# TensorE's seven-pass loop of the recurrence written out, its value transposes moved behind the round's first product, and each stage's semaphores cleared inside the next stage

## The reference, cut to what matters

```python
def step(S, inp):                      # chunks of tokens
    qt, kt, vt, gt = inp
    G = jnp.cumsum(gt, axis=2)
    o_inter = jnp.einsum('bhtk,bhkv->bhtv', qt * jnp.exp(G), S)
    A = jnp.einsum('bhtk,bhtsk->bhts', qt, decay * kt[:, :, None, :, :])
    o = o_inter + jnp.einsum('bhts,bhsv->bhtv', A, vt)
    S = jnp.exp(G_last)[..., None] * S + jnp.einsum('bhsk,bhsv->bhkv', kt * jnp.exp(G_last - G), vt)
    return S, o
```

## Time and profile before

| | |
|---|---|
| runs, us | 2702.21, 2703.32, 2710.44 |
| profiled execution, its own time | 2706.89 us |
| its span, first to last instruction | 2705.1 us |
| mean granted TensorE clock | 0.954 |
| busy: PE, PEld (weight load) | 2440.8 us, 2263.8 us |
| busy: DVE (VectorE), ACT (ScalarE), POOL | 1252.1, 1035.6, 432.7 us |
| stage hgrn2, first product to the first of the next stage | 563.1 to 1410.8 us |

### The profile page before, as it was taken

One profiled execution on the slowest core, in us unless ns is written; L12 is line 12 of the kernel. 1 busy time (PEld: TensorE's weight loads), 2 busy tenths in 40 slices (PEclk: granted clock), 3 DMA queues, 4 the chain that ended last, 5 costly groups with the idle time before them and its releaser, 6 DMA issues. The chain is left out here.

```text
span 2705.1 us, 59385 instructions
## 1 busy us (share of the span) xinstructions
PE 2440.8 (90%) x25397; PEld 2263.8 (84%) x25397; DVE 1252.1 (46%) x1639; ACT 1035.6 (38%) x1505; POOL 432.7 (16%) x282
## 2 busy tenths in 40 slices
PE   5999899999999999999948996982899999999993
PEld 4999899999899899899948996971788888888882
DVE  4123210015555555555542112027567676677673
ACT  4222221113333233233322112132566666676663
POOL 1221131111111111111103113102111212111110
PEclk9999999999999999999969997986899999999997
DMA  3112231211101101101014225135487887878774
GB/s 117 32 36 79 97 104 50 68 41 41 35 22 46 35 17 51 35 17 51 19 43 143 76 71 214 31 118 233 167 315 281 301 306 276 306 285 315 271 275 173
DMA packets 183594, 351.02 MB, mean 130 GB/s; under 512 B 10512, under 2 KB 110864, under 8 KB 183440
## 3 DMA queue, kind: packets, MB, share of 16 engines
q1 hardware_dynamic: 177296, 327.78, 34.1%
q0 software_dynamic: 6144, 20.98, 3.0%
HBM read 301.54 MB, written 47.19 MB: 129 GB/s over the span
## 5 line engine op out<-in xcount | busy, mean ns | idle before, releaser
L1598 DVE TENSOR_TENSOR ex_w_lo<-ex_raw,ex_w_hi 128x1024 fp32r<-128x1024 f32 x377 | 450.1, 1222 | 150.8 <-ACT ex_w_hi L1590 147.6
L1590 ACT ACTIVATE ex_w_hi<-ex_raw 128x1024 fp32r<-128x1024 f32 x384 | 398.9, 1057 | 143.9 <-PE ex_out L1832 122.0
L176 PE MATMUL hg_proj<-trunk_h_hi,hg_w_hi 128*128 128x320 f32 x768 | 251.7, 328 | 16.8 <-issue 16.8
L177 PE MATMUL hg_proj<-trunk_h_lo,hg_w_hi 128*128 128x320 f32 x768 | 243.9, 318 | 0.3 <-issue 0.2
L178 PE MATMUL hg_proj<-trunk_h_hi,hg_w_lo 128*128 128x320 f32 x768 | 243.4, 317 | 0.0
L1830 PE MATMUL ex_out<-ex_w_hi,ex_x_hi 128*128 128x512 f32 x512 | 205.6, 402 | 2.2 <-DVE ex_x_lo L1616 2.2
L1831 PE MATMUL ex_out<-ex_w_hi,ex_x_lo 128*128 128x512 f32 x512 | 200.5, 392 | 0.0
L1832 PE MATMUL ex_out<-ex_w_lo,ex_x_hi 128*128 128x512 f32 x512 | 200.2, 391 | 0.0
L176 PEld LDWEIGHTS hg_proj<-trunk_h_hi,hg_w_hi 128*128 128x128 f32 x768 | 150.3, 196 | 20.2 <-issue 18.2
L176 PE MATMUL hg_proj<-trunk_h_hi,trunk_w_hi 128*128 128x320 f32 x512 | 161.9, 316 | 5.3 <-POOLq L201 5.3
L177 PE MATMUL hg_proj<-trunk_h_lo,trunk_w_hi 128*128 128x320 f32 x512 | 158.8, 310 | 0.0
(11 more groups left out here) (329 smaller groups left out, 6108.8 us busy)
## 6 DMA issues: line engine op xcount, KB each, us to landing
ex_raw<-in_w_exp_gate_dram SPq DMA_DIRECT2D x32, 2048.0 KB, 11.4
ex_raw<-in_w_exp_up_dram SPq DMA_DIRECT2D x32, 2048.0 KB, 12.4
ex_raw<-in_w_exp_down_dram SPq DMA_DIRECT2D x32, 2048.0 KB, 17.8
trunk_w_raw<-in_w_in_dram SPq DMA_DIRECT2D x48, 512.0 KB, 4.2
hg_w_raw<-in_w_in_dram SPq DMA_DIRECT2D x16, 512.0 KB, 4.7
ya<-gm_ya SPq DMA_DIRECT2D x8, 640.0 KB, 3.4
m_a<-ma_m SPq DMA_DIRECT2D x8, 640.0 KB, 3.4
yb<-hg_Kt_b SPq DMA_DIRECT2D x8, 640.0 KB, 5.1
```

The source lines that it names most:

```text
L176: nc.tensor.matmul(out, self.hi[s][:, k, :], x_hi[:, k, c], start=(k == 0), stop=False)
L177: nc.tensor.matmul(out, self.hi[s][:, k, :], x_lo[:, k, c], start=False, stop=False)
L1590: nc.scalar.activation(w_hi[u % RING][:], src, ACT.Copy).then_inc(s["w_hi_ready"], 1)
L1598: ops.tensor_tensor(w_lo[u % RING][:], src, w_hi[u % RING][:].bitcast(F32), ALU.subtract).then_inc(s["w_lo_ready"], 1)
```

## The change

1. TensorE's `Fori` over heads 0 to 6 becomes a Python loop: its seven passes stand one behind the other in the program. The other engines keep their loops.
2. `pe_values` and `act_values` go from the end of a round (head g+1) to the place behind the first product group of the next (head g). The wait for `v` moves from DIAG to level 6 (INNER), where the bank area that held the transposed values is first written again; DIAG waits for the query tile instead.
3. A stage's semaphores are no longer cleared behind its own block but at the end of POOL's program in the following block, and are returned to the allocator after that block; those of the last stage are cleared at the end of the program, as before.

```diff
@@ class Stage @@
+    used = []
     def __exit__(self, *a):
-        if self.sems and a[0] is None:
-            for sem in self.sems:
-                self.nc.gpsimd.sem_clear(sem)
-                self.nc.release_semaphore(sem)
+        if a[0] is None:
+            Stage.used += self.sems
         return self.ctx.__exit__(*a)
+    @contextmanager
     def block(self):
-        return self.nc.Block()
+        before, Stage.used = Stage.used, []
+        with self.nc.Block() as block:
+            yield block
+            @block.gpsimd
+            def _(pool):
+                for sem in before:
+                    self.nc.gpsimd.sem_clear(sem)
+        for sem in before:
+            self.nc.release_semaphore(sem)
@@ hgrn2, pe_step @@
             if j == DIAG:
-                pe.wait_ge(s["v_ready"], g + 1)
+                W.moved(pe, g, TQ)
...
+                if j == INNER:
+                    pe.wait_ge(s["v_ready"], g + 1)
@@ hgrn2, pe_round (act_round likewise, with act_values) @@
                     W.multiply(nc, pe, *tiles[n // PARTS], n % PARTS, h_hi, h_lo)
+                if g is not None and n == 0:
+                    pe_values(pe, g)
                 if g is not None and n < STEPS:
                     pe_step(pe, g, n)
-            if tiles[-1][1] == TI:
-                pe_values(pe, tiles[-1][0])
@@ hgrn2, block.tensor @@
-                with pe.Fori(0, HEADS - 1) as g:
+                for g in range(HEADS - 1):
                     pe_round(pe, tiles_with(g), g)
```

More of the change, by code:

```diff
@@ L14 @@
-from contextlib import ExitStack
+from contextlib import ExitStack, contextmanager
 import concourse.bass as bass
@@ L71, in __exit__, with clear_all @@
     def __exit__(self, *a):
-        if self.sems and a[0] is None:
-            for sem in self.sems:
-                self.nc.gpsimd.sem_clear(sem)
-                self.nc.release_semaphore(sem)
+        if a[0] is None:
+            Stage.used += self.sems
         return self.ctx.__exit__(*a)
+    def clear_all(self):
+        for sem in Stage.used:
+            self.nc.gpsimd.sem_clear(sem)
+            self.nc.release_semaphore(sem)
+        Stage.used = []
     def sb(self, name, shape, dt=F32):
@@ L675, in act_round @@
                     act_move(act, r, t, n % PARTS)
+                if g is not None and n == 0:
+                    act_values(act, g)
                 if g is not None:
                     act_gla(act, g, n)
-            if tiles[-1][1] == TI:
-                act_values(act, tiles[-1][0])
         def pool_round(pool, tiles):
@@ L2051, in build @@
         norm_out(nc, C, x3, I["final_g"], y_prompt, y_sample)
+        top.clear_all()
 _INS = ["x_prompt", "x_sample", "norm1_g", "w_in", "a_vnorm_g", "a_spatial_w", "a_spatial_b", "b_lb_logits",
```

## The result

The changed kernel takes **2667.76 us** (median of four runs, 2664.53 to 2671.03), the kernel before, run beside it, 2706.8 us. The ratio is 0.9857, with a 95% interval of 0.9831 to 0.9882: faster by some 39 us, where 45.9 us were predicted. The forecast was a median of 2657 us, in a range of 2648 to 2668 us. The profiled execution took 2670.59 us, 36.3 us less than that of before (2706.89). The direction was right; the gain was about a sixth smaller than the working gave.

A forecast was written before the change was run, and what follows sets the result against it. TensorE's queue was taken to bound the recurrence's rounds, with jumps costing pauses and low clock. 35.1 + 4.8 - 0.5 + 6.5 = 45.9 us off a 2703.3 us median gave 2657 us, range 2648 to 2668 us.

The forecast's parts named there:

- What bounds the kernel: Recurrence rounds are as long as TensorE's queue; each of six jumps back costs a code pause (16.8 us in all) and low clock.
- Part 1: Recurrence loop written out: six rounds fall from 612.81 to 577.74 us, 35.1 us gained, bounds 16.8 and 38.3.
- I cost the fetching in line at nothing: Written-out recurrence: products hide the code fetch, as in the first round; unhidden, one more 2.8 us pause per round.
- Part 2: Transposes behind the round's first product: TensorE's 5.6 us of waits for ScalarE go, 4.8 us gained after removing double counting.
- The 0.5 us taken back for the last round: Last recurrence round: ScalarE's later work delays VectorE's key levels, no product covers levels from the fourth on; 0.5 us lost.
- Part 3: Clears moved at stage borders: SP's 7.5 us of waits for POOL's credit at five starts shrink, 6.5 us gained.
- The clock falls on its own: Rival: low clock comes from long dense load, so only the pauses go in the recurrence; 27.6 us gained, 2676 us; chance 0.06.
- ScalarE's later copy: Rival: the later copy of v reaches TensorE in each recurrence round, giving back up to 10 us; 2667 us; chance 0.07.
- The pause stays: Rival: pause belongs to the round's start, or in-line code comes too late; 35 us back, 2692 us; chance 0.03.
- The experts' loop is pushed out: Rival: written-out code makes the experts' 13 jumps back pause, 5.9 us each, 76 us; slower, 2734 us; chance 0.02.
- The clears held nobody: Rival: the loads' landings, not the clears, held the five stage starts; 6.5 us less gain, 2664 us; chance 0.05.

## Why the prediction was right and wrong

**What bounds the kernel: right.** TensorE's queue sets the round, and the pause with the stretch of low clock behind it was the cost of the jumps. With nothing in the way a round is 95.45 us, a little under the 96.29 - 0.57 = 95.72 us of the working.

**Part 1, the step that failed: "I cost the fetching in line at nothing".** It rested on the first round, which runs through cold code at full clock. But that was one place of the code in its blocks, and the written-out loop has seven. It was also another code: there the transposes and DIAG had a product between them, and part 2 put them together. With the loop written out alone two rounds were over 96.5 us (98.25 and 97.27), with part 2 the fourth is at 100.45; how much of that is the denser code and how much the other place isn't separated. Seven clean rounds would be 668.15 us; the changed kernel took 675.81. These 7.7 us are mostly the pauses of rounds 1, 4 and 7 and the low clock behind that of round 4, and they are nearly the whole miss of the stage: clean rounds would have gained 41.1 us where parts 1 and 2 gave 39.4, the real ones gained 33.5. Three kernels with other places changed which rounds pause and for how long, one put it in every second round, three took it away (one of them at another cost). The text named the price of such a case (a pause of 2.8 us in each round) and put it outside the sum and into a rival of 0.03; it was never a matter of all rounds or none.

**Part 2: right in the sum, wrong as a part.** The waits went. VectorE's first key level starts 1.1 us later behind DIAG than before: 2.97 us, where it was 1.83 (DIAG of that round at 727.45 us, and the earlier trace rows); 1.2 us later was predicted. TensorE's waits didn't grow by it. This is the row after the change, in the round whose DIAG starts at 721.78 us:

```profile
724.75 0.75 DVE L718 TENSOR_TENSOR hg_K_even<-hg_K_odd,hg_f_f 128x320 f32<-128x320 f32 x1 [6.27 <-ACT hg_K_even L731]
```

The 0.5 us taken back for the last round wasn't needed. But the part alone is worth 27 us, because without the wait ahead of the jump the jump's own cost falls by more than half. The working counted the pause wholly to part 1; for the whole change this made no difference, for anyone who makes only one part it would.

**Part 3: about the right size, and unsettled.** The waits of the starts fell by 0.4 (gm), 0.7 (hg), 1.6 (ma) and 1.8 us (mb), and wo's by 1.2: 5.7 us of the 6.5. What comes last now is ScalarE's credit, where the text had named TensorE's and SP's. In the time the clears are worth 2 us by the ratio (interval from nothing to 5) when moved alone, and 8.8 us when put back into the changed kernel (at least 4 by the runs' ends). 5.7 us lies between. The profiles lean to the larger value: take from each span the stretch from hg's first product to mb's, and the 3.3 and 12.9 us that the increments cost at the start of two kernels. Then the four kernels with the clears in the old place take 1857.4 to 1865.2 us and the fourteen others 1851.1 to 1856.6. That is 6.9 us apart in the mean, where the shorter waits in this part explain 3.9. What the rest is stays open. That the clears in their new place hide, and that the end of the experts doesn't feel them, was right: the experts take 812.4 us as before.

**The rivals.** *The clock falls on its own*: no; in the seven rounds of all 18 profiles it was low only in or shortly behind a pause of 1.97 us or more. *ScalarE's later copy*: its number (2667) was the right one, its mechanism not, as the kernel with the copy later still shows. *The pause stays*: in part true, for another reason than the two that it gave. *The experts' loop is pushed out*: no, it runs 550 us of 550 without a gap. *The clears held nobody*: against it stand 5.7 us of waits and the 8.8 us.

**The range** was 2648 to 2668 us, and the median came out at 2667.76, inside by a quarter of a us, with two of the four runs above. That is luck and no support for the working; the interval of the ratio gives 2661 to 2675 us beside the 2706.8 of before. The centre was 11 us low. 3.5 us of that are the kernel before, whose median with a fourth run is 2706.8 and not 2703.3, and 6.9 us are the gain that was missed. Its upper end took in the clears and part of ScalarE's case; the cost of code in line should have been a term with a bound from the one pause that the trace had (2.92 us) and the stretch behind it, 5.9 us a time, in some of the rounds.

## What to carry to other kernels

Straight code is not free where it is dense: where a few hundred short instructions pass in 3 us, the next block of code can be late, and the pause moves when instructions are added ahead of it (10 to 33 here). So compare a written-out loop round by round; one odd round, with "issue" as the reason and a packet on the instruction queue, is this. And before a jump is written out, see what stands ahead of it: moving the transposes, and their semaphore wait with them, away from the jump gained 27 us with the loop kept, as much as writing it out, and both together, the clears included, 38.

## What the runs showed of the hardware

- A backward jump cost 2.41 to 3.00 us of pause with a semaphore wait shortly ahead of it (two profiles, twelve jumps) and 0.91 to 1.38 us without one (two profiles, twelve jumps). The fetch behind it, from the start of its packet to the first product, took 2.6 to 3.1 us in both.
- In straight code TensorE stood up to 3.67 us for its next block of code, whose packets never started less than 3.0 us apart; some of these pauses were followed by 3.4 us of low clock (6.8 in one profile), some not: 98.85 us the round with 3.14 us of pause and none, 100.45 with 3.38 and one.
- Idle semaphore increments on TensorE: five behind a product of 24 matmuls cost nothing, 22 or 23 cost some 0.9 us (6.6 us in a round with seven such blocks); at the program's start 33 cost nothing, 100 cost 3.3 us and 163 cost 12.9 us.
